# Decay and rate projections of both directions in alternating row halves, and the two heads' inversion products back to back

## The reference, cut to what matters

```python
for d, (ow, oa) in enumerate(((OFF_WF, OFF_AF), (OFF_WB, OFF_AB))):
    lw = (w0[d] + jnp.tanh(z[..., ow:ow + DECAY_LORA]) @ w_up[d]).astype(jnp.float32)
    decay = jnp.exp(-jnp.exp(-jax.nn.softplus(-lw) - 0.5))
    a = jax.nn.sigmoid((a0[d] + z[..., oa:oa + ICLR_LORA] @ a_up[d]).astype(jnp.float32))
    k_d = kf * (1.0 + (a - 1.0) * k_a.astype(jnp.float32))
    dirs.append((to_heads(decay), to_heads(k_d), kk * to_heads(a)))
...
def step(S, inp):
    w_t, k_t, v_t, kk_t, kka_t = inp[:5]
    sa = jnp.einsum('bhvk,bhk->bhv', S, kk_t)
    S = (S * w_t[:, :, None, :] - sa[..., None] * kka_t[:, :, None, :]
         + v_t[..., None] * k_t[:, :, None, :])
```

## Time and profile before

| | |
|---|---|
| median of 3 runs | 4067.24 us (4062.73 to 4070.47) |
| profiled execution | 4079.55 us, span 4077.7 us |
| TensorE busy | 3880.4 us, 95% of the span, 51352 passes |
| VectorE, ScalarE, GpSimd busy | 1687.0, 1146.1, 551.5 us |
| TensorE's share of the chain that ended last | 90% |
| mean granted TensorE clock | 0.986 of full speed |
| ScalarE table loads | 106, 136.0 us |

### The profile page before, as it was taken

One profiled execution on the slowest core, in us unless ns is written; L12 is line 12 of the kernel. 1 busy time (PEld: TensorE's weight loads), 2 busy tenths in 40 slices (PEclk: granted clock), 3 DMA queues, 4 the chain that ended last, 5 costly groups with the idle time before them and its releaser, 6 DMA issues.

```text
span 4077.7 us, 111806 instructions
## 1 busy us (share of the span) xinstructions
PE 3880.4 (95%) x51352; PEld 2546.8 (62%) x51352; DVE 1687.0 (41%) x2721; ACT 1146.1 (28%) x2003; POOL 551.5 (14%) x436
## 2 busy tenths in 40 slices
PE   7899999999999999999999988999998999999998
PEld 3566666666555555655555556666666556678887
DVE  2555566664862111322231254555555422122232
ACT  3444444442122000200000344444444221021001
POOL 0000000000032221122232000000000023213443
PEclk8999999999999999999999999999999999999999
DMA  5000000000333223211112300000010253242224
GB/s 205 25 9 24 25 25 25 25 22 28 108 131 104 93 88 95 79 61 62 52 62 73 123 25 9 23 23 23 23 34 21 68 194 114 83 144 92 85 89 129
DMA packets 76337, 277.40 MB, mean 68 GB/s; under 512 B 8672, under 2 KB 13024, under 8 KB 75488
## 3 DMA queue, kind: packets, MB, share of 16 engines
q1 hardware_dynamic: 67968, 235.96, 18.1%
q10 hardware_dynamic: 6624, 29.04, 1.9%
q0 software_dynamic: 1280, 5.24, 0.3%
HBM read 256.58 MB, written 13.63 MB: 66 GB/s over the span
## 4 chain that ended last, share of the span: by engine, by line
PE 90%; ACT 4%; issue 3%; DVE 2%; DMA 1%; POOL 0%; ACTq 0%; DVEq 0%; SPq 0%; POOLq 0%
PE psum L1156 17%; PE psum L1670 16%; PE psum L1040 12%; PE psum L741 11%; PE psum L1467 9%; PE psum L1602 6%; PE psum L1052 5%; PE psum L1562 3%; PE psum L1625 2%; PE psum L1188 2%; PE psum L732 2%; PE psum L1000 2%; DMA ring<-w_stream_in 1%; PE psum L1018 1%; PE psum L921 1%
## 5 line engine op out<-in xcount | busy, mean ns | idle before, releaser
L1156 PEld LDWEIGHTS psum<-arena 32*32 32x32 f32 (+3 forms) x40512 | 697.6, 117 | 375.4 <-issue 301.4
L1156 PE MATMUL psum<-arena 32*32 32x32 f32 (+4 forms) x40512 | 790.8, 208 | 105.4 <-issue 73.7
L1040 PE MATMUL psum<-arena,ring 128*128 128x512 f32 (+1 forms) x1408 | 573.1, 523 | 2.5 <-ACT arena L1858 1.6
L741 PE MATMUL psum<-arena,ring 128*128 128x512 f32 (+1 forms) x1264 | 463.1, 524 | 3.8 <-DVE arena L2552 3.8
L741 PEld LDWEIGHTS psum<-arena,ring 128*128 128x128 f32 x1264 | 238.8, 191 | 230.3 <-issue 200.7
L1670 PE MATMUL psum<-arena 128*128 128x384 f32 (+1 forms) x1344 | 368.6, 433 | 0.0
L1040 PEld LDWEIGHTS psum<-arena,ring 128*128 128x128 f32 x1408 | 239.2, 191 | 142.0 <-issue 115.5
L1670 PEld LDWEIGHTS psum<-arena 128*128 128x128 f32 x1344 | 255.4, 190 | 106.4
L2991 POOL DMA_DIRECT2D ya_spill<-arena x16 | 8.8, 550 | 1995.2 <-DVE arena L2552 1995.2
L1670 PE MATMUL psum<-arena,ring 128*128 128x384 f32 (+1 forms) x1008 | 278.5, 433 | 0.0
L1670 PEld LDWEIGHTS psum<-arena,ring 128*128 128x128 f32 x1008 | 191.6, 190 | 79.5
(11 more groups left out here) (175 smaller groups left out, 4428.6 us busy)
## 6 DMA issues: line engine op xcount, KB each, us to landing
ring<-w_stream_in SPq DMA_DIRECT2D x440, 512.0 KB, 3.8
x_spill<-arena ACTq DMA_DIRECT2D x2, 3072.0 KB, 8.7
arena<-x_spill ACTq DMA_DIRECT2D x16, 384.0 KB, 6.5
arena<-ya_spill ACTq DMA_DIRECT2D x6, 768.0 KB, 6.0
ring<-w_stream_in ACTq DMA_DIRECT2D x8, 512.0 KB, 6.4
arena<-x_in ACTq DMA_DIRECT2D x1, 3072.0 KB, 14.3
arena<-ups_in SPq DMA_DIRECT2D x16, 192.0 KB, 2.4
ya_spill<-arena POOLq DMA_DIRECT2D x8, 384.0 KB, 6.3
```

Source lines behind the costliest of these rows:

```text
L741: mm = eng.matmul(psum[0:lhs[k].shape[-1], tile, a - off:b - off], lhsT=lhs[k], rhs=rhs[k][:, a:b], start=(k == 0), stop=(k == len(lhs) - ...
L1040: mm = pe.matmul(bank(j, z=b - a), lhsT=w[k], rhs=hs[k][:, a:b], start=(k == 0), stop=(k == KT - 1))
L1156: return pe.matmul(out, lhsT=lhs, rhs=rhs, start=start, stop=stop, skip_group_check=True)
```

## The change

Decay and rate are cut into products of 128 tokens, and the two directions take turns: each product of direction 0 (upper 64 rows of the array) is followed by the same tokens of direction 1 (lower 64 rows), in two different banks. They come in three groups of eight instead of eight single tiles: `first` (decay, latent), `both` (decay, context, and rate, context) and `last` (rate, latent). In turn 0 the groups have banks of their own (2 to 7), in the other turns all use banks 0 and 1, for which `hold` names the last gate. The gates of ScalarE and the shift of R on VectorE are reordered to fit. The strings of TensorE for turns 1 and 2 to 7 are new in both layers, with the `s` of two heads side by side.

```diff
-UP_ORDER = ((0, 0), (1, 1), (1, 0), (0, 1))
+UP_ORDER = dict(lw=((0, 0), (1, 0), (0, 1), (1, 1)), la=((0, 1), (1, 1), (0, 0), (1, 0)))
+UP_GROUPS = dict(first=(("lw", 0, 0),), both=(("lw", 1, 0), ("la", 1, 256)), last=(("la", 0, 0),))
+UP_BANK = dict(first=2, both=4, last=6)
...
 WEAVE.update((("PE", 0, t), (
-    "xxdsxsdssdxxssxdxxdddxsddsdddsxddddsddxdsddddsddsddsdsddsxddsdddsddsdddsdddsddddsddsdxddsdddsdsdssss"
+    "xxdsxsdssdxxssxdxxdddxssdddddssxdddddxdddssdssddddddddssdssdxdddddssddddddssdddsdxddsdddsdsdsssssddss"
...
+                def up_group(t, group):
+                    if t >= KT:
+                        return
+                    g = KT * l + t
+                    pe.wait_ge(ups[g % 3], 16 * (g // 3 + 1))
...
+                    name, half, at = UP_GROUPS[group][-1]
+                    for d in DIRS:
+                        hold(up_bank(t, group, d), (sw if name == "lw" else sa).at(g, UP_ORDER[name].index((d, half))))
+                    for name, half, at in UP_GROUPS[group]:
+                        (a, b), n, src, ev = HALVES[half], "lw la".split().index(name), LW if name == "lw" else LA, lw if name == "lw" else la
+                        for c in range(a, b, P):
+                            for d in DIRS:
+                                mm = pe.matmul(bank(up_bank(t, group, d), a=at + c - a, z=at + c - a + P), lhsT=ups_block(g, n, side(d)),
+                                               rhs=slot(src, c, c + P)[side(d)], start=True, stop=True, skip_group_check=True)
+                                if c + P == b:
+                                    mm.then_inc(ev.sem, 1)
+                    yield
...
                     yield from k_tiles(t, 1, 2, 4)
-                    yield from decay_tile(t, 0)
                     yield from k_tiles(t, 1, 4, 6)
-                    yield from decay_tile(t, 1)
                     yield from k_tiles(t, 1, 6, 8)
-                    yield from decay_tile(t, 2)
+                    yield from up_group(t, "first")
                     yield from r_tiles(t, 0, 0, 2)
-                    yield from decay_tile(t, 3)
                     yield from r_tiles(t, 0, 2, 4)
-                    yield from rate_tile(t, 0)
                     yield from r_tiles(t, 0, 4, 6)
-                    yield from rate_tile(t, 1)
                     yield from r_tiles(t, 0, 6, 8)
+                    yield from up_group(t, "both")
...
                     yield from r_tiles(t, 1, 6, 8)
+                    yield from up_group(t, "last")
...
                     yield from raw_k_half(0)
+                    yield from raw_k_half(1)
                     yield from decay_gate(0)
                     yield from decay_gate(1)
-                    yield from raw_k_half(1)
-                    yield from decay_gate(2)
-                    yield from decay_gate(3)
+                    yield from raw_r_half(0)
...
                     yield from k_shift(1)
+                    yield from r_shift(0)
                     if prep:
                         for d in DIRS:
                             dve.wait_ge(*sw.at(g, 3))
...
-                    yield from r_shift(0)
```

More of the change, by code:

```diff
@@ L645, in state_sum, with up_bank, up_result @@
             return bank((6 if n < 8 else 4) + d, rows, n % 8 * C, n % 8 * C + C)
+        def up_bank(t, group, d):
+            return d + (0 if t else UP_BANK[group])
+        def up_result(t, name, j):
+            d, half = UP_ORDER[name][j]
+            group, at = [(k, at) for k, parts in UP_GROUPS.items() for n, h, at in parts if (n, h) == (name, half)][0]
+            a, b = HALVES[half]
+            return bank(up_bank(t, group, d), a=at, z=at + b - a)
         def wk(c, rows=slice(0, P), a=0, b=P):
```

56 lines of the change are left out of this document (23 added, 33 removed).

## The result

The changed kernel takes 4220.77 us (median of 4 runs, 4210.41 to 4228.17), the kernel before, measured beside it, 4067.74 (4062.73 to 4070.47). The ratio is 1.0376, 95% interval 1.035 to 1.0402: 153 us slower, where 59 had been predicted. The direction was right, the size was out of the range.

What follows compares the result with a forecast made beforehand. Instruction supply, some 128 passes per 3.84 us, was taken to bound the inversions. Twelve inversions (61 us), two first ones (7) and turn 0 twice (-9) gave +59 us on 4067: 4126 us, own range 4095 to 4150, wider range 4050 to 4170.

Steps and rivals of the forecast that it cites:

- The supply as a lower bound: In inversions, TensorE's instructions come in pieces of some 128 passes, no less than about 3.84 us apart, and TensorE waits.
- Thirty-two more passes: Each inversion has 24 products instead of 8, so 32 more passes: 1.0 us more of instruction supply.
- Bunching: Per inversion, supply stands still up to 3.2 us during eight dense products; with the 1.0 us for passes, 3.6 taken.
- The clock: More idle time in inversions makes falls of the granted clock common: 0 to 4 us each, 1.5 taken.
- the 6.8 us removed: TensorE's own work falls 6.8 us per inversion through alternating products and fewer shape changes, but comes back as idle time.
- Waits, taken at 0: Waits on ScalarE's gates and VectorE's decay scan in the inversions are covered by other work, so cost 0.
- The gates at the R products: R products stand behind ScalarE's gates in turns other than 0: 0 taken, 33 us in all without cover.
- First inversions: Turn 1 of each layer has less dense work to bunch and some context products: 3.5 us more each.
- Turn 0: No scan and no supply limit there, so cheaper tiles and fewer shape changes save 4.5 us, twice: 9 us.
- The sum: Twelve inversions at 3.6 + 1.5 give 61 us, two first ones 7, turn 0 twice -9: +59 us.
- The third rival: ScalarE's and VectorE's waits are not covered and the clock falls in nearly every inversion: 4171 us; chance 0.15.

Runs made afterwards that it cites:

- the mended first layer: First layer of the changed kernel with calls set apart and the first norm maximum between VectorE's scans: six inversions 342.3 us, whole kernel 1.0147 of before.
- the whole-width kernel: Changed kernel with its three groups in products of the full 512 or 256 tokens, 8 a turn instead of 24: 1.0344 of the kernel before.
- the turn-0 kernel: Kernel before with the three alternating groups, banks 2 to 7 and their orders only in turn 0 of each layer: 4048.49 us, 0.996 of before.
- the first two experiments: Changed kernel with the inversion calls set apart again: 1.0105 of the kernel before; kernel before with only its calls bunched in pairs: 1.0464.

## Why the prediction was right in direction and wrong in size

- **The supply as a lower bound** held where the calls are bunched: 56 us of unread work for 7 us of time, and the mended first layer 3.65 us less busy at the same length. It was too strong as a law of the kernel before: half of 48 us of work taken from the tiles came back as time, and 128 more passes cost 3.0 us, not 3.84. Nor is 3.84 us the least distance of two pieces: 3.48 was seen, and 3.64 as the mean of a whole inversion. My reason, equal lengths of the two layers at unequal work, was a coincidence in part: L1 is 320 to 339 us at identical order.
- **Thirty-two more passes, +1.0 us an inversion**: the whole-width kernel is 13 us faster than the changed one, 14 were predicted; but the difference is within the intervals, so the term is not shown.
- **Bunching, 3.6 us an inversion**: this is the term that failed. With the clock that goes with it, it was put at 3.6 - 1.0 + 1.5 = 4.1 us and measured as 9.2 (110 us over 12, calls set apart against changed kernel); some 1.6 of these are norm waits that went with it. Its mechanism was half right. The stalls come 128 passes apart, and not more than one piece is in store behind the dense piece, as predicted; but the loss was priced as the time that the supply stands still in that piece, and splitting it won nothing. An inversion is idle for 15.3 and 13.1 us, and most of that lies in the runs of small calls ("issue" waits of 147.5 us in all, 73.7 before). Why such runs cost this much, and not only where, stays open.
- **The clock, 1.5 us an inversion**: failed with it. TensorE's busy time did not fall by the 6.8 us removed (55.35 to 55.38) and rose by 8.4 us where nothing but the bunching was changed. My "one more fall in each two or three inversions" became a granted clock of 0.79 to 0.93 in all twelve. Even the upper end, 4 us, was too low, as it counted one fall in an inversion.
- **Waits, taken at 0**: failed. I looked at ScalarE's gates and at the scan between subtraction and transpose, and not at what stands behind the scans: the norm maximum, on which the second norm tile waits for its bank. With the scans later and the norm tiles earlier it cost 35.3 us of waits, and removing 20.7 of them 35 us of time. The gates at the R products, which I did price, cost almost nothing (4.6 us in the second layer).
- **First inversions**: 3.5 us each predicted, 6.9 and 7.6 measured; no run takes them apart.
- **Turn 0**: 9 us predicted, 2.4 + 5.8 = 8.2 measured in the changed kernel and 6.3 in the turn-0 kernel; right.
- **The sum**: 12 x 5.1 should have been 12 x 12.0. That it came out on the slower side is no luck, as the first two experiments show the bunching to be the main cost. The third rival (more waits and clock, 4171 us) named the right kinds of cost, though not the norm maximum, and was still 50 us short.

## What to carry to other kernels

Where small products are fed at a limited pace, spread them: runs of 96 passes with a product or two between them were the faster order here, runs of 192 the slower, at pieces of 128. Work saved elsewhere gave half at best. When a tile is moved later, follow its result through the next engine's queue to whatever stands behind it, above all tiles that share a bank. And a change that shifts the instruction count ahead of such a stretch can move the time by about 0.25% (10 us here, the cost of the shifting products taken off) with no cause of its own; shift the kernel before by the same count before crediting or blaming the edit.

## What the runs showed of the hardware that I had not expected

- Where the pieces of the instruction stream begin changed six inversions of identical order by 12 to 18 us out of 339, in single executions; by the runs it is about 10.
- A gap of 2.16 us in front of dense work was followed by 9.68 us instead of 7.13 for the eight products behind it, at a granted clock of 0.73. The runs don't separate the gap from the run of small products ahead of it.
- A product of 128x128 weights with only 32 streamed columns costs 3.76/16 = 0.23 us. In a run of 32 it was 9.88/32 = 0.31, with the clock falling to 0.50 during the run, although TensorE was idle neither before it nor in it. So idle time is not needed for a fall, and such a product is no cheap filler.
